# Recurrence of a block on one core: the projection of the answers goes between joins and transitions, that of the values into the scan

## The chip, the cores and the metric

The kernel runs on one core of a Trainium2 chip. The metric is device time in microseconds (us) of one launch, the median of the runs. All data is float32; a float32 matmul stands as two instructions in the trace.

## The reference

Two transformer blocks follow each other on 512 tokens of width 1024. The first mixes in a context of 256 tokens, with a recurrence of RWKV kind, a state-space branch and 16 experts; the second has a retention and a delta-rule mixer and 16 experts again. The change concerns only the recurrence of the first block, which runs in both directions over 16 heads of 64:

```python
r, k, v, xw, xa, xg = jnp.split(u, RW_SPLITS, axis=-1)      # u: projected tokens, after centred_shift
...
kk = (k * p['rw_kk']).astype(F32).reshape(b_, n, RW_HEADS, RW_HEAD)
kk = kk * lax.rsqrt(jnp.maximum(jnp.sum(kk * kk, axis=-1, keepdims=True), 1e-12))
k_eff = k[:, :, None] * (1 + (a - 1) * p['rw_ka'])
...
def step(s, inp):
    r_t, w_t, k_t, v_t, kk_t, a_t = inp
    sa = jnp.einsum('bhvk,bhk->bhv', s, -kk_t)
    s = s * w_t[:, :, None, :] + sa[..., None] * (kk_t * a_t)[:, :, None, :] + v_t[..., None] * k_t[:, :, None, :]
    return s, (jnp.einsum('bhvk,bhk->bhv', s, r_t) if with_output else None)
```

`r` is called the answers here, `k` the keys, `v` the values. The answers are needed for the 512 tokens alone, keys and values for context and tokens, 768 in all.

## The kernel before

The function `rwkv` works on 8 pairs of heads (PAIRS, 128 channels each). The 768 positions of a pair are cut into 12 chunks of 64 for each of the two directions: 24 units. The engines run programs of their own, written out by hand, and wait for each other by semaphores; nothing schedules them. One turn of the main loop computes the recurrence of pair c ("core") and prepares pair p = c + 1 ("prep"); a first turn, c = -1, only prepares, the last, c = 7, only computes. So seven turns do both.

On TensorE a turn goes through these phases:

- near: inner products of keys in each unit (L608), then the values turned (L622), the bonus (L746), and the answer of the pair before turned (`turn_y`, L616).
- keys 0 to 5: for each four units products with the answers (L635, L641) and transposes (L648, L651). Between them stand the projections of the next pair's keys, its small low-rank products (L577, L578) and `modulate` 0 to 3 (L598), which multiplies the conditioning vector into weights that two slots (`rw_mod_w`) bring in by turns, all eight summed in PSUM bank 1. VectorE meanwhile inverts the triangles by substitution (L987, L988) and masks the products of each four units (L970, L973, L975).
- the values' part (L660), `join_first` (L670), `join_second` (L681, L683), which put 32-wide inverses together into 64-wide ones with ScalarE's copies (L914 to L934) between them, `modulate` 4 to 7, and the sums for the key norm (`kk_sums`, L584).
- transitions: for q = 0 to 5 products `wu` (L692) and `mr` (L703), each followed by one matmul of a projection; at q = 2 also `kk_spread` (L591). Then `new_part` (L713), the gate's product (L820).
- the scan, steps 1 to 11, each in both directions: TensorE multiplies the state with the step's transition (L723), VectorE makes the new state (L1045), and TensorE's next step waits for it. Beside them stand products that only add to the answer (L729 in steps 1 to 8, L734 from step 4).

A projection is eight matmuls (k = 0 to 7) of a 128x128 piece of `rw_w` with 512 tokens or 256 context positions (L571). `project_part(j, part, k0, k1)` does k0 to k1 of it; j is 0 for answers, 1 for keys, 2 for values, part 0 for tokens, part 1 for context. ScalarE copies the finished sum with a scale (`centre`, L842), VectorE adds the neighbours on both sides (`neighbours`, L997, L998), and `fill` (L1027 to L1031) multiplies keys, gated keys and answers with the decay factors that ScalarE made in `factors` (L848 to L853). The factor of the answers stands in `e1`. `exponents` (L1003 to L1007) makes the exponents, `write_keys` (L1013 to L1020) the effective keys. near of the next turn waits for both `fill`s and the values' neighbours.

There is one buffer `rw_w` for the projections' weights. SyncE loads the next pair's as soon as all of `project_part(2, 1, ...)` is done (L512).

## Time and profile before

| what | us |
|---|---|
| median of 3 runs (lowest, highest) | 4329.08 (4328.28, 4329.16) |
| the profiled execution's own time | 4327.74 |
| its span | 4326.0 |
| TensorE busy, of the span | 3495.1 (81%) |
| VectorE busy | 1618.1 (37%) |
| ScalarE busy | 774.8 (18%) |
| the recurrence, from 133 to 1076 | 943 |
| TensorE busy in it | 830.4 |
| VectorE busy in it | 622.4 |
| ScalarE busy in it | 354.1 |

The recurrence takes 943 us of the span. TensorE's near phases start at 303.15, 415.99, 528.82 and so on, one every 112.8 us. The share of the whole page is an average over stages with other limits, so everything that matters for this change is read from one such turn, here mostly the one that ends at 528.82. In it TensorE works nearly without a break, and the question is what stands behind each of its few pauses.

### The profile page before, as it was taken

The page shows a single profiled execution, that of the slowest core. Times are in us where ns is not written, and L with a number is a line of the kernel's source. Part 1 is how long each engine was busy: PE and PEld are TensorE (multiplying, and loading weights), DVE is VectorE, ACT ScalarE, POOL GpSimd, SP SyncE. Part 2 cuts the span into 40 slices and gives each one's busy share as a digit, 9 for nine tenths or more (in the row PEclk, how much of TensorE's full clock was granted, in tenths as well). Part 3 has the DMA queues.
Part 4 walks back from the last instruction along what each step waited for, and adds up shares of the span by engine and source line. Part 5 has one row for each costly group of instructions (what it writes and reads, how often), then busy time and mean ns, then how long its engine had stood idle before and what let it go on. Part 6 is the DMA issues. An engine that isn't in the chain of part 4 may idle for free. (4 is left out here: it accounts for less than half of the span.)

```text
span 4326.0 us, 57405 instructions
## 1 busy us (share of the span) xinstructions
PE 3495.1 (81%) x24436; PEld 2129.8 (49%) x24436; DVE 1618.1 (37%) x3303; ACT 774.8 (18%) x1501; POOL 51.8 (1%) x72
## 2 busy tenths in 40 slices
PE   5799999997879888689956778858797888758994
PEld 2466666666545555434433322334444444347883
DVE  2466666665465674600122000022314132251112
ACT  1233433442121111200010000011212112100101
POOL 0000000000000000000000000000000000000000
PEclk7899999998889899899967999969898999858997
DMA  3121122212010000122036999731102010137884
GB/s 132 45 70 61 64 69 70 70 54 79 30 52 36 29 29 30 60 105 97 39 149 254 428 428 428 303 119 42 74 6 80 39 41 1 63 137 283 328 326 160
DMA packets 98023, 531.13 MB, mean 123 GB/s; under 512 B 33568, under 2 KB 36112, under 8 KB 72992
## 3 DMA queue, kind: packets, MB, share of 16 engines
q1 hardware_dynamic: 90912, 503.06, 29.8%
q0 software_dynamic: 4608, 16.78, 1.1%
q10 hardware_dynamic: 2304, 8.39, 0.5%
q8 instruction: 156, 2.56, 0.2%
q14 instruction: 43, 0.35, 0.0%
HBM read 500.85 MB, written 27.34 MB: 122 GB/s over the span
## 5 line engine op out<-in xcount | busy, mean ns | idle before, releaser
L1930 PE MATMUL ex_ps<-ex_ring,ex_xs 128*64 128x512 f32 x1024 | 242.7, 629 | 62.5 <-DMA ex_ring<-expert_slabs_in 59.4
L571 PE MATMUL rw_ps<-hT,rw_w 128*128 128x512 f32 (+1 forms) x640 | 256.9, 531 | 16.2 <-DMA rw_w<-rw_slabs_in 15.9
L2667 PEld LDWEIGHTS ge_ps<-ge_xeT,ge_ring 128*128 128x128 f32 x2048 | 232.7, 193 | 10.5 <-issue 10.5
L2667 PE MATMUL ge_ps<-ge_xeT,ge_ring 128*128 128x128 f32 x2048 | 233.0, 276 | 2.9 <-DVE ge_xeT L2725 2.9
L2164 PE MATMUL mh_ps<-mh_w,xmT 128*128 128x512 f32 x512 | 221.5, 593 | 8.6 <-ACT mh_sg L2187 8.6
L1315 PE MATMUL sg_ps<-hTp,sg_w 128*128 128x512 f32 x384 | 179.5, 623 | 27.9 <-PEq L61 27.9
L1930 PEld LDWEIGHTS ex_ps<-ex_ring,ex_xs 128*64 128x64 f32 x1024 | 88.2, 145 | 216.5 <-issue 214.7
L2164 PEld LDWEIGHTS mh_ps<-mh_w,xmT 128*128 128x128 f32 x512 | 96.9, 190 | 132.5 <-issue 120.5
L571 PEld LDWEIGHTS rw_ps<-hT,rw_w 128*128 128x128 f32 x640 | 112.5, 191 | 98.9 <-issue 72.9
L2155 PE MATMUL mh_ps<-xmT,mh_w_ahead 128*128 128x512 f32 x256 | 121.0, 637 | 22.4 <-PEq L61 22.4
L1315 PEld LDWEIGHTS sg_ps<-hTp,sg_w 128*128 128x128 f32 x384 | 76.5, 201 | 117.4 <-issue 116.4
L1930 PE MATMUL ex_ps<-ex_ring,ex_hidT 128*64 128x512 f32 x512 | 119.2, 620 | 16.2 <-DMA ex_ring<-expert_slabs_in 15.1
L1610 PE MATMUL mg_ps<-mg_pb,ybT 128*128 128x512 f32 x256 | 114.0, 604 | 17.4 <-DMA mg_pb<-proj_b_in 17.4
L2729 DVE TENSOR_TENSOR ge_hid<-ge_hid,ge_ps 128x512 f32<-128x512 f32 x16 | 11.0, 688 | 291.5 <-PE ge_ps L2667 291.5
L1989 DVE TENSOR_TENSOR ex_hid<-ex_hid,ex_ps 128x512 f32<-128x512 f32 x16 | 11.0, 687 | 291.5 <-PE ex_ps L1930 291.5
L1672 PE MATMUL po_ps<-po_w,po_mT 128*128 128x512 f32 x256 | 112.0, 600 | 4.2 <-DMA po_w<-w_out_in 4.2
L2676 PE MATMUL ge_ps<-ge_ring,ge_hid 128*128 128x512 f32 x256 | 113.7, 597 | 0.8 <-issue 0.8
L1359 DVE SCALAR_TENSOR_TENSOR sg_acc<-sg_ps,sg_par,sg_acc 128x510 f32<-128x510 f32 (+3 forms) x176 | 110.5, 628 | 6.3
L1325 PE MATMUL sg_ps<-sg_wz,hTp 128*128 128x512 f32 x256 | 110.5, 592 | 0.0
L2164 PE MATMUL mh_ps<-mh_w_ahead,xmT 128*128 128x512 f32 x256 | 110.5, 592 | 0.0
L1443 PEld LDWEIGHTS sg_ps<-sg_xdt,sg_diff 128*128 128x128 f32 x512 | 65.2, 197 | 64.2 <-DVE sg_diff L1518 60.4
L2155 PEld LDWEIGHTS mh_ps<-xmT,mh_w_ahead 128*128 128x128 f32 x256 | 52.1, 205 | 89.3 <-issue 89.3
(571 smaller groups left out, 5606.8 us busy)
## 6 DMA issues: line engine op xcount, KB each, us to landing
ex_ring<-expert_slabs_in SPq DMA_DIRECT2D x96, 2048.0 KB, 19.8
ge_ring<-expert_slabs_in SPq DMA_DIRECT2D x48, 2048.0 KB, 12.4
rw_mod_w<-mod_w_in SPq DMA_DIRECT2D x64, 384.0 KB, 4.0
rw_mod_w<-ada_in SPq DMA_DIRECT2D x64, 256.0 KB, 3.3
mh_w_ahead<-head_slabs_in SPq DMA_DIRECT2D x8, 2048.0 KB, 10.1
mh_w<-head_slabs_in SPq DMA_DIRECT2D x8, 2048.0 KB, 10.1
rw_w<-rw_slabs_in SPq DMA_DIRECT2D x8, 1536.0 KB, 6.3
sg_w<-xbc_slabs_in SPq DMA_DIRECT2D x4, 3072.0 KB, 9.9
```

The source lines that it names most:

```text
L571: mm = pe.matmul(where[j, part], w[:, k, P * j:P * j + P], tokens, start=k == 0, stop=k == KC - 1)
L1315: mm = pe.matmul(ps[:, bank, :], w[:, k, P * b:P * b + P], hTp[:, k, :], start=k == 0, stop=k == KC - 1)
L1325: mm = pe.matmul(ps[:, 6 + c % 2, :], hTp[:, k, P * c:P * c + P], wz[:, k, :], start=k == 0, stop=k == KC - 1)
L1359: link(dve.scalar_tensor_tensor(out[:, lo:hi], src[:, lo + j - 2:hi + j - 2], par[:, b, j:j + 1], out[:, lo:hi], ALU.mult, ALU.add))
L1443: mm = pe.matmul(ps[:, 7 * (c % 2), v], diff[:, n % ND, P * h:P * h + P], xdt[:, d, c, v], start=n % 4 == 0 and h == 0, stop=n % 4 == 3 an ...
L1610: mm = pe.matmul(ps[:, b + j, :], src[:, k, off + P * t:off + P * t + P], w[:, k, :], start=k == 0, stop=k == nk - 1)
L1672: mm = pe.matmul(ps[:, 4 + t, :], mT[:, k, P * t:P * t + P], w[:, n, k, :], start=k == 0, stop=k == KC - 1)
L1930: mm = pe.matmul(ps[halves[j], bank, :], src[:, k, halves[j]], ring[:, (n + j) % RING, k, :], start=k == 0, stop=k == KC - 1)
L2155: mm = pe.matmul(ps[:, b, :], w[0][:, k, P * b:P * b + P], xmT[:, k, :], start=k == 0, stop=k == KC - 1)
L2164: mm = pe.matmul(ps[:, 4 + t, :], xmT[:, k, P * t:P * t + P], w[1 + n // 4][:, k, :], start=k == 0, stop=k == KC - 1)
L2667: mm = pe.matmul(ps[:, 2 + 2 * (j % 2) + n, P * f:P * f + P], w[:, k, P * f:P * f + P], xeT[:, j, k, :], start=k == 0, stop=k == KC - 1)
L2676: mm = pe.matmul(ps[:, 6 + h, :], hid[:, j, f, :], w[:, f, 512 * h:512 * h + 512], start=f == 0, stop=f == FB - 1)
```

## The change

The projections of the next pair are dealt out differently on TensorE. The work is the same; only the order differs.

- The answers' projection, before 3 matmuls after keys 4, 2 before `join_first` and 3 before `join_second`, is now 2 before `join_second` and 6 in the transitions, one for each q.
- The values' projection over the tokens, before 6 in the transitions and 2 after the gate's product, is now one matmul in each of the scan steps 1 to 8. That over the context, before two in each of the steps 1 to 4, is now one in each of the steps 1 to 8.
- The wait for `mod_done` (VectorE has taken bank 1 away) stands ahead of the scan instead of ahead of the transitions, since bank 1 is where the values' tokens are summed.
- VectorE: the answers' neighbours come after scan step 1 instead of in the transitions; `fill` is cut in two, `fill` and `fill_answers`. The answers of direction 0 are filled after step 2, `write_keys(p, 1)` stands after step 3 instead of 2, both fills of direction 1 after step 8 instead of after step 10, the values' neighbours after steps 9 and 10 instead of 5 and 7.
- ScalarE: the answers' `centre` stands after the last `keep_wu`, and `factors(p, 1)` waits until the answers of direction 0 are filled, since it writes `e1` anew.

```diff
@@ TensorE, the main loop
                     if core:
                         keys(c, 4)
                         modulate(c, 2)
-                    if prep:
-                        project_part(0, 0, 0, 3)
-                    if core:
                         keys(c, 5)
                         modulate(c, 3)
                         value_part(c)
                         modulate(c, 4)
-                    if prep:
-                        project_part(0, 0, 3, 5)
-                    if core:
                         join_first(c)
                         modulate(c, 5)
                     if prep:
-                        project_part(0, 0, 5, 8)
+                        project_part(0, 0, 0, 2)
...
                         wu(c, 0)
                         wu(c, 1)
-                        pe.wait_ge(s.mod_done, c + 1)
                     for q in range(6):
...
-                            project_part(2, 0, q, q + 1)
+                            project_part(0, 0, q + 2, q + 3)
...
                     if prep:
-                        project_part(2, 0, 6, 8)
+                        if core:
+                            pe.wait_ge(s.mod_done, c + 1)
                         pe.wait_ge(s.kk_done, p + 1)
                     for step in range(1, RW_NCH):
                         if core:
                             scan_step(c, step)
-                        if prep and step <= 4:
-                            project_part(2, 1, 2 * step - 2, 2 * step)
+                        if prep and step <= 8:
+                            project_part(2, 0, step - 1, step)
+                            project_part(2, 1, step - 1, step)
@@ ScalarE
                     else:
+                        act.wait_ge(s.filled, 2 * p + 1)
                         act.activation(e1[:, :], ee[:, :], ACT.Exp, scale=KAPPA).then_inc(s.first_exp, 1)
...
                     if prep:
-                        centre(p, 0, 0, rc[:, :], ps[:, 2, :])
                         factors(p, 0)
                     if core:
                         for q in range(3, 6):
                             keep_wu(c, q)
                     if prep:
+                        centre(p, 0, 0, rc[:, :], ps[:, 2, :])
                         factors(p, 1)
@@ VectorE
-                    dve.tensor_tensor(bk[:, u, 64:P], token_cut(aas[:, d, :]), token_cut(bf[:, :]), ALU.mult)
+                    dve.tensor_tensor(bk[:, u, 64:P], token_cut(aas[:, d, :]), token_cut(bf[:, :]), ALU.mult).then_inc(s.keys_filled, 1)
+
+                def fill_answers(p, d):
+                    ul = slice(RW_NCH * d + RW_CC, RW_NCH * d + RW_NCH)
                     dve.wait_ge(s.shifted_r, p + 1)
-                    dve.tensor_tensor(kr[:, ul, 64:P], token_cut(rc[:, :]), token_cut(rf[:, :], RW_CC), ALU.mult).then_inc(s.filled, 1)
+                    dve.tensor_tensor(kr[:, ul, 64:P], token_cut(rc[:, :]), token_cut(e1[:, :], RW_CC), ALU.mult).then_inc(s.filled, 1)
...
                     if prep:
-                        neighbours(p, 0, 0, rc[:, :], ps[:, 2, :], SEQ)
-                        dve.sem_inc(s.shifted_r, 1)
                         dve.wait_ge(s.norm_spread, p + 1)
...
                         scan_step(c, 1)
+                    if prep:
+                        neighbours(p, 0, 0, rc[:, :], ps[:, 2, :], SEQ)
+                        dve.sem_inc(s.shifted_r, 1)
+                    if core:
                         scan_step(c, 2)
+                    if prep:
+                        fill_answers(p, 0)
+                    if core:
+                        scan_step(c, 3)
                     if prep:
                         write_keys(p, 1)
                     if core:
-                        for step in range(3, 6):
+                        for step in range(4, 9):
                             scan_step(c, step)
+                    if prep:
+                        fill(p, 1)
+                        fill_answers(p, 1)
+                    if core:
+                        scan_step(c, 9)
                     if prep:
                         neighbours(p, 2, 0, vc[:, CTX:NT], ps[:, 1, :], SEQ)
                     if core:
-                        scan_step(c, 6)
-                        scan_step(c, 7)
+                        scan_step(c, 10)
                     if prep:
                         neighbours(p, 2, 1, vc[:, 0:CTX], ps[:, 3, 256:512], CTX)
                         dve.sem_inc(s.shifted_v, 1)
-                    if core:
-                        for step in range(8, 11):
-                            scan_step(c, step)
-                    if prep:
-                        fill(p, 1)
```

TensorE from `modulate` 2 (L598) to the transitions, in a turn that does both, before and after. The L571 rows are projections; xN counts matmuls.

```order
 L651 MATMUL rw_ps<-consts,rw_kr 64x64 x8
 L598 MATMUL rw_ps<-rw_mod_w,rw_cond 32x320 x4
-L571 MATMUL rw_ps<-hT,rw_w 128x512 x3
 L635 MATMUL rw_ps<-rw_kr,rw_bk 64x128 x8
 L641 MATMUL rw_ps<-rw_kr,rw_bk 64x64 x8
```

```order
 L660 MATMUL rw_ps<-rw_tk 64x64 x48
 L598 MATMUL rw_ps<-rw_mod_w,rw_cond 32x320 x4
-L571 MATMUL rw_ps<-hT,rw_w 128x512 x2
 L670 MATMUL rw_ps<-rw_low,rw_mid 32x32 x48
 L598 MATMUL rw_ps<-rw_mod_w,rw_cond 32x320 x4
-L571 MATMUL rw_ps<-hT,rw_w 128x512 x3
+L571 MATMUL rw_ps<-hT,rw_w 128x512 x2
 L681 MATMUL rw_ps<-rw_diag,rw_mid 32x32 x24
```

Six projection matmuls of 512 columns leave the stretch between keys 4 and `join_second`. In the changed kernel the scan's lines are the same on TensorE (L723, L729, L734). Its start there, from the gate's product (L813 of the changed kernel) to step 3:

```order
L813 MATMUL rw_ps<-xg,rw_gw 128x512
L723 MATMUL rw_ps<-rw_kx,rw_tk 64x64 x2
L729 MATMUL rw_ps<-rw_tk 64x64 x4
L723 MATMUL rw_ps<-rw_kx,rw_tk 64x64 x2
L729 MATMUL rw_ps<-rw_tk 64x64 x4
L571 MATMUL rw_ps<-hT,rw_w 128x512
L571 MATMUL rw_ps<-hT,rw_w 128x256
L723 MATMUL rw_ps<-rw_kx,rw_tk 64x64 x2
L729 MATMUL rw_ps<-rw_tk 64x64 x4
L723 MATMUL rw_ps<-rw_kx,rw_tk 64x64 x2
L729 MATMUL rw_ps<-rw_tk 64x64 x4
```

Each of the steps 1 to 8 is now followed by a matmul of 512 and one of 256 columns, where steps 1 to 4 had two of 256. VectorE in the scan of the kernel before, from the states of steps 3 to 5 (two each, so x6) to the answer's statistics (L1126):

```order
L1045 SCALAR_TENSOR_TENSOR rw_kx<-rw_ps,rw_fac,rw_kx 128x64 x6
L997 SCALAR_TENSOR_TENSOR rw_v<-rw_ps,rw_par,rw_v 128x511
L998 SCALAR_TENSOR_TENSOR rw_v<-rw_ps,rw_par,rw_v 128x511
L1045 SCALAR_TENSOR_TENSOR rw_kx<-rw_ps,rw_fac,rw_kx 128x64 x4
L997 SCALAR_TENSOR_TENSOR rw_v<-rw_ps,rw_par,rw_v 128x255
L998 SCALAR_TENSOR_TENSOR rw_v<-rw_ps,rw_par,rw_v 128x255
L1045 SCALAR_TENSOR_TENSOR rw_kx<-rw_ps,rw_fac,rw_kx 128x64 x6
L1027 TENSOR_TENSOR rw_kr<-rw_kk,rw_q 128x12x64
L1028 TENSOR_TENSOR rw_bk<-rw_sg,rw_e 128x12x64
L1029 TENSOR_TENSOR rw_bk<-rw_a,rw_e 128x12x64
L1031 TENSOR_TENSOR rw_kr<-rw_r,rw_e 128x8x64
L1126 TENSOR_REDUCE rw_st<-rw_ps 128x8
```

The end of the scan on VectorE in the changed kernel, from step 4 on (L1043 is the state's line there, L1022 to L1029 the fills, L993 and L994 the neighbours):

```order
L1043 SCALAR_TENSOR_TENSOR rw_kx<-rw_ps,rw_fac,rw_kx 128x64 x10
L1022 TENSOR_TENSOR rw_kr<-rw_kk,rw_q 128x12x64
L1023 TENSOR_TENSOR rw_bk<-rw_sg,rw_e 128x12x64
L1024 TENSOR_TENSOR rw_bk<-rw_a,rw_e 128x12x64
L1029 TENSOR_TENSOR rw_kr<-rw_r,rw_e 128x8x64
L1043 SCALAR_TENSOR_TENSOR rw_kx<-rw_ps,rw_fac,rw_kx 128x64 x2
L993 SCALAR_TENSOR_TENSOR rw_v<-rw_ps,rw_par,rw_v 128x511
L994 SCALAR_TENSOR_TENSOR rw_v<-rw_ps,rw_par,rw_v 128x511
L1043 SCALAR_TENSOR_TENSOR rw_kx<-rw_ps,rw_fac,rw_kx 128x64 x2
L993 SCALAR_TENSOR_TENSOR rw_v<-rw_ps,rw_par,rw_v 128x255
L994 SCALAR_TENSOR_TENSOR rw_v<-rw_ps,rw_par,rw_v 128x255
L1129 TENSOR_REDUCE rw_st<-rw_ps 128x8
```

The four fills now stand between the states of step 8 and step 9, the values' neighbours behind the states of steps 9 and 10.

## Rows read from the trace of the kernel before

**Rows 1.** Waits of TensorE, 416 to 529: total us, times, longest.

```profile
PE rw_ps L635 <- DVE rw_kr L1152: 2.5, 1, 2.5
PE rw_ps L723 <- DVE rw_kx L1045: 2.1, 3, 0.9
```

**Rows 2.** Timeline of TensorE to the transitions: start, duration, [idle before, releaser].

```profile
459.50 2.84 PE L571 MATMUL rw_ps<-hT,rw_w 128*128 128x512 f32 x6
...
469.90 1.98 PE L571 MATMUL rw_ps<-hT,rw_w 128*128 128x512 f32 x4
...
474.13 2.84 PE L571 MATMUL rw_ps<-hT,rw_w 128*128 128x512 f32 x6
...
481.09 1.96 PE L692 MATMUL rw_ps<-rw_kx,rw_xt 64*64 64x128 f32 x32
...
489.47 1.60 PE L591 MATMUL rw_ps<-consts,rw_kk 128*128 128x128 f32 x12
```

**Rows 3.** Timeline of ScalarE in the joins.

```profile
473.57 0.58 ACT L921 COPY rw_mid<-rw_ps 32x512 f32<-32x512 f32 x1 [1.65 <-PE rw_ps L670]
...
475.31 2.11 ACT L925 COPY rw_xt<-rw_diag 32x384 f32<-32x384 f32 x4
...
478.56 1.95 ACT L934 COPY rw_xt<-rw_ps 32x384 f32<-32x384 f32 x4 [0.18 <-PE rw_ps L683]
```

**Rows 4.** Timeline of VectorE, last mask of the keys.

```profile
463.48 0.69 DVE L973 TENSOR_TENSOR rw_tk<-rw_ps,consts 128x512 f32<-128x512 f32 x1 [2.36 <-PE rw_ps L635]
```

**Rows 5.** Landing of the loads of rw_mod_w, whole run.

```profile
DMA to landing us min/median/max: 2.6/3.7/8.1
```

**Rows 6.** Timeline of VectorE in the transitions.

```profile
490.26 0.74 DVE L997 SCALAR_TENSOR_TENSOR rw_r<-rw_ps,rw_par,rw_r 128x511 f32<-128x511 f32 x1
...
491.93 0.75 DVE L1083 SCALAR_TENSOR_TENSOR rw_kk<-rw_k,rw_par,rw_ps 128x512 f32<-128x512 f32 x1
...
499.15 0.68 DVE L1031 TENSOR_TENSOR rw_kr<-rw_r,rw_e 128x512 f32<-128x512 f32 x1
...
505.07 1.88 DVE L1101 TENSOR_TENSOR rw_kx<-rw_ps,rw_fac 128x512 f32<-128x512 f32 x3
```

**Rows 7.** Timeline of TensorE, gate, scan and next near.

```profile
507.05 1.10 PE L820 MATMUL rw_ps<-xg,rw_gw 128*128 128x512 f32 x2 [1.80 <-issue]
...
509.79 0.33 PE L723 MATMUL rw_ps<-rw_kx,rw_tk 64*64 64x64 f32 x4
...
510.63 1.13 PE L571 MATMUL rw_ps<-hT,rw_w 128*128 128x256 f32 x4
...
516.33 0.33 PE L723 MATMUL rw_ps<-rw_kx,rw_tk 64*64 64x64 f32 x4 [0.75 <-DVE rw_kx L1045]
...
517.40 1.13 PE L571 MATMUL rw_ps<-hT,rw_w 128*128 128x256 f32 x4
...
528.82 2.42 PE L608 MATMUL rw_ps<-rw_kr,rw_bk 64*64 64x64 f32 x48 [2.87 <-DVE rw_kr L1031]
```

**Rows 8.** Timeline of VectorE in the scan.

```profile
512.63 0.95 DVE L1013 TENSOR_TENSOR rw_sg<-rw_kk,rw_a 128x768 f32<-128x768 f32 x1
...
515.99 0.48 DVE L1045 SCALAR_TENSOR_TENSOR rw_kx<-rw_ps,rw_fac,rw_kx 128x64 f32<-128x64 f32 x2
...
525.47 0.95 DVE L1027 TENSOR_TENSOR rw_kr<-rw_kk,rw_q 128x768 f32<-128x768 f32 x1
...
528.68 0.68 DVE L1126 TENSOR_REDUCE rw_st<-rw_ps 128x8 f32<-128x512 f32 x1
```

**Rows 9.** Stretches: length, busy (instructions) of PE, PEld, DVE, ACT, POOL, PEclk, DMA, GB/s.

```profile
392.00:416.00 24.00, 17.19 (x312) 12.77 (x306) 16.11 (x37) 3.39 (x6) 0.00 (x0) 1.00 0.19 68
...
416.00:430.00 14.00, 11.47 (x243) 10.42 (x243) 10.28 (x26) 9.39 (x22) 0.00 (x0) 0.77 0.12 27
```

**Rows 10.** Timeline of VectorE in the first turn, which only prepares.

```profile
169.17 0.17 DVE L1070 TENSOR_SCALAR rw_norm<-rw_ps 128x12 f32<-128x12 f32 x1 [2.42 <-PE rw_ps L584]
...
171.33 0.75 DVE L997 SCALAR_TENSOR_TENSOR rw_r<-rw_ps,rw_par,rw_r 128x511 f32<-128x511 f32 x1 [1.49 <-ACT rw_r L842]
```

5 lines of the change are left out of this document (2 added, 3 removed).

## The prediction, written before the changed kernel ran

> **What bounds the recurrence now.** I read first the share of busy time by stretch, then TensorE's waits, then the timelines of the three engines side by side through one turn. TensorE is the engine to watch: it is busy for 830 of the 943 us, VectorE for 622, ScalarE for 354. The turn takes 112.8 us from near to near (415.99 to 528.82, the last in [rows 7]). TensorE pauses in it before near (2.87, until VectorE's last fill), before the gate (1.80) [rows 7], before keys 0 (2.5) and in the scan (2.1 in three pieces) [rows 1]. That is some 9.3 of 112.8 us. Moving work on TensorE can only win by filling such a pause, and loses where it opens one. Two parts of the turn matter: the stretch from keys 5 to the transitions, which loses work, and the scan, which takes it.
>
> **Part 1, keys and joins.** Three projection matmuls between keys 4 and 5 go. They start at 459.50 and take 2.78 (three matmuls are x6 and 2.84, of which 0.06 overlaps) [rows 2]. Does VectorE hold keys 5 back instead? Its last mask waited 2.36 for TensorE's product [rows 4], so it is early; the mask that keys 5 need was done at about 458.2. So everything to the values' part comes 2.78 earlier, and VectorE 2.36. Before `join_first` two matmuls go (1.92, from 469.90), before `join_second` one of three (0.92 of 2.77, from 474.13) [rows 2]. TensorE could reach `join_second` 2.78 + 1.92 + 0.92 = 5.62 earlier.
>
> ScalarE is the next to be late. Its copies between the joins follow the values' part, which moves by 2.78, and only the wait of 1.65 before L921 gives way [rows 3]: `join_first` comes 4.70 earlier, so L921 starts 4.40 earlier (at 469.17, right behind the copies in front of it). That is 2.78 plus all but 0.03 of 1.65. L925 is then done with the rest at 4.40, and L934, which waited another 0.18, at 4.58 earlier: it ends at 480.51 - 4.58 = 475.93. The first `wu`, before at 481.09 [rows 2], needs it and starts near 476.0. **Gain 5.0**, and TensorE pauses about 0.5 there that it did not before. The bounds: 5.62 if ScalarE were no limit; 2.78 if L921's wait gave nothing.
>
> `modulate` 7 gets less time for its weights: its slot is reloaded once `modulate` 5 is done (about 469.4) and it is due at 473.5. With the second issue 0.5 later and a landing of 3.7 [rows 5] it is in at 473.6, and a delay of up to 0.5 is lost in ScalarE's limit anyway. I take nothing; the price is worked out below.
>
> **Part 2, transitions.** The six fillers stay six, of the same size. The wait for bank 1 costs nothing at either place, VectorE takes it before the first `wu`. What changes is VectorE's chain to the gate. The answers' neighbours leave it (490.26 to 491.93), but the key's norm cannot start before `kk_spread` is through, 489.47 + 1.5 = 491.0 [rows 2, 6], so 0.9 is won; the answers' fill leaves too, 499.15 to 499.87, 0.7 [rows 6]. VectorE is 1.6 earlier at its last three products. The third needs `new_part`, which ended at 507.05 - 1.80 = 505.25 [rows 7], and takes a third of 1.88 [rows 6], 0.65. So the gate's product starts at 505.25 + 0.1 + 0.65 + 0.1 = 506.1 in the old time, **gain 0.9**, with 1.6 and 0 as bounds.
>
> **Part 3, the scan.** In the old kernel it starts at 509.79 and near at 528.82 [rows 7]: 19.03. In the new one two matmuls of 512 no longer stand ahead of it (their time, 1.8, is counted here), so it starts at 507.05 - 5.0 - 0.9 + 0.93 (the gate) = 502.1.
>
> Step lengths on TensorE: 0.84 for steps 1 to 3 (509.79 to 510.63), 1.07 for step 4 (516.33 to 517.40), 0.98 for 5 to 8 [rows 7] (0.98 from the starts of later steps in the same timeline). Together 7.5. Each is followed by one matmul of 512, 0.91, and one of 256, 0.53 (517.40's four instructions are followed by the next step 1.07 later), so 8 x 1.44 = 11.5. Step 9 is reached at 19.0.
>
> VectorE beside it, from the scan's start: the state of a step is ready 0.45 + 0.28 after TensorE starts it. Neighbours of the answers, 1.6, between 1.0 and 2.6: step 2's product comes at 2.3 and its state is asked for at 2.75, no delay. `write_keys`, 3.36 (512.63 to 515.99 [rows 8]), from 5.65 to 9.0: the state of step 4 is then late, and TensorE may go on with step 5 at 9.0 + 0.34 (515.99 to 516.33 [rows 7, 8]) = 9.34. It gets there at 9.36. So this stall of 0.75 [rows 7] is just covered; if it isn't, it costs a few tenths. The same for the stalls of 0.9 and 0.4 after steps 6 and 8, whose causes move to the end.
>
> The end is VectorE's. Step 8 starts at 16.6, its states are made by 17.75, then the four fills 3.21 (525.47 to 528.68 [rows 8]) until 20.95. States of step 9, 0.4; values' neighbours, 1.57 (as the answers', [rows 6]); states of step 10, 0.4; the second neighbours, 1.0 with its signal 1.1. Near starts at 24.5. TensorE was done with step 9 at about 19.5: of the last 5.0 us it works one. Near comes at 502.1 + 24.5 = 526.6 against 528.82. So of the 5.9 of parts 1 and 2 and the 1.8 of the moved pair, the scan takes 5.4 back: **gain 2.3 a turn**. Bounds from the two sides: the scan without any pause, 19.0 + 1.5 for steps 9 to 11 = 20.5, gives 6.3; with the old pauses of 2.1 and 2.87 kept and the new ones on top, 26.5, it gives 0.3.
>
> ScalarE's new wait (`e1`) is over after step 2, and it has 2.5 us of factors to make before the fills at 17.75; cover 11 us. Queued behind it are only the values' copies, due at 18.7. SyncE: the load of the projections' weights starts when the context's values are done, 19.0 instead of 9 after the scan's start. It lands in about 6.3 us, near 25.5, and its first reader stands 14 us after near's start. No cost. POOL has nothing moved.
>
> **The first turn** only prepares and is VectorE's. Its wait of 2.42 for the key sums goes, since six matmuls no longer stand ahead of them; the 1.49 before the answers goes as well [rows 10], but VectorE must now wait some 2.5 for the norm to be spread. **Gain 1.5** (0 to 3.9). The last turn has no projections: nothing.
>
> Sum: 7 x 2.3 + 1.5 = 17.6.
>
> **The clock.** The stretch from 416 to 430 ran at a granted 0.77, the 24 us before at 1.00 [rows 9]: twice a turn TensorE falls to 1.2 GHz, once behind the pause of 2.87 and once behind that of 2.5, not behind 1.80. At most 0.23 x 14 = 3.2 us a turn are lost so. Now the pause before near is in pieces, about 1.9, 1.5 and 0.5, none as long as those that the drop followed, though close together; and the turn's phases shift. I take 0.6 a turn, 4 in all, between -1.6 (a third drop) and 3.2 a turn. The Trainium skill ("TensorE: Matmul & The Clock Gate", HAM oscillation) puts the return to the half clock down to long gaps between matmuls, and by that alone the drop before near would be gone: 1.6 x 7 = 11 us instead of 4. The same page (A second HAM failure mode) speaks against that: frequent short idles between groups also make the clock swing. No row of this trace has such a broken pause, so the sum keeps to the value near the lower end.
>
> The profiled execution took 4327.7, 1.3 under the median. 4327.7 - 17.6 - 4 = 4306.1 for it, **4307.5** at the median.
>
> **Rivals.**
> - *The clock gives more.* The drop behind the broken pause goes in all turns, and that behind keys' 2.5 in some: 1.6 to 2.6 a turn, 4329 - 17.6 - 15 = 4297. For it: no piece is as long as 2.5. Against: TensorE works only 1 of 5 us there. Chance 0.17.
> - *The joins don't shrink as far.* ScalarE and VectorE hold each other, 4.0 instead of 5.0 is won, `write_keys` just stalls step 5, a clock drop moves: gain 1.1 a turn, 4329 - 9 = 4320. Chance 0.12.
> - *Nothing comes of it.* The scan is a chain between two engines, and a projection in each step only makes it longer; what was won in front goes into the end, where VectorE has 7 us of work behind step 8 and TensorE nothing. If the tail is 2 us longer than I work out, the turn stays at 112.8: 4328. Against: the rows give each link of the tail. Chance 0.07.
> - *Slower, by the weights of `modulate` 7.* They decide from a landing of 6.4 us on (3.6 of room, 0.5 of slack, 2.3 of gain). The longest landing of all was 8.1, the median 3.7 [rows 5]. At 8.1 in every turn, 4.0 late, a turn loses 1.7: 4329 + 12 - 1.5 = 4339. Against: TensorE never waited more than tenths for them. Chance 0.05.
>
> **How the numbers follow.** The forecast has 0.59, its own range 4301 to 4315. The range of 8 in 10 goes from 4297, the clock's rival, to 4321, the weaker joins. 0.2% of 4329 is 8.7 us, about what a measurement of this kernel tells from none. Faster by more: below 4320.4, the forecast, the clock's rival and half of the weaker joins, less a little for the unknown: 0.83. Within: 0.11. Slower: 0.06.
>
> **What would show it.** In the changed profile near should follow near after about 110 us. The pause of 0.5 before the first `wu` (on ScalarE's L934), the gate's of 0.9, no pause in steps 1 to 8, then about 1.9 and 1.5 before steps 10 and 11 and 0.5 before near, all released by VectorE; the granted clock between near and keys 1 over 0.77. The forecast is wrong if step 5 or later steps stall, if `modulate` 7 waits for a DMA, or if the joins are less than 4 us nearer to keys 5.

## The result, and the profile after

The changed kernel takes 4332.6 us at the median of 20 runs (4320.6 to 4340.8). The kernel before, run beside it 20 times, takes 4324.8 (4319.0 to 4332.0). The ratio is 1.0017, with a 95% interval of 1.0009 to 1.0025: slower by 0.17%, where 4307.5 was forecast. The difference is small, but the interval leaves one out, and a repetition gave the same ratio.

| profiled execution | before | after |
|---|---|---|
| own time / span, us | 4327.7 / 4326.0 | 4336.5 / 4334.8 |
| mean granted clock of TensorE | 0.893 | 0.887 |
| to the first near | 193.9 | 193.8 |
| first near to eighth near (seven turns) | 786.0 | 786.4 |
| eighth near to the end | 3346.1 | 3354.6 |

In the seven turns that do both nothing was won. The last turn of the recurrence and the stages behind it, whose instructions are the same, took 8.5 us more; I come back to those at the end. The turns of before are alike (112.7 to 112.8, the first 109.2). Those of after are not. Each piece below is read from the starts of the first near, first `wu`, gate and next near in TensorE's timeline; "pause" is a pause there behind which no wait of before stands.

| turn | near to first `wu` | `wu` to gate | gate to near | turn | new pauses in the joins |
|---|---|---|---|---|---|
| before | 65.1 | 25.96 | 21.77 | 112.8 | none |
| 1 | 56.7 | 24.91 | 26.07 | 107.6 | 0.5 DMA |
| 2 | 62.5 | 26.48 | 26.07 | 115.1 | 0.86 and 0.17 unreleased, 0.5 DMA |
| 3 | 61.4 | 24.90 | 26.08 | 112.4 | 0.47 unreleased |
| 4 | 62.6 | 27.36 | 26.07 | 116.0 | 1.83 unreleased |
| 5 | 60.2 | 24.90 | 26.08 | 111.2 | 0.87 DMA |
| 6 | 60.3 | 24.90 | 26.08 | 111.3 | 0.5 DMA |
| 7 | 61.8 | 24.91 | 26.08 | 112.8 | 0.6 unreleased |

"Unreleased" means that the profile shows nothing that the engine waited for (its word is "issue"). The pause before the gate carries this word too, in both kernels [rows 7]; it is not counted here.

First TensorE's waits between 100 and 1090 us (total, times, longest). L813 is the gate, L723 and L734 are the scan's products, L608 is near, L598 is `modulate`, L670 and L683 are the joins. DVEq is VectorE's sequencer; at L1125 it signals that the values' neighbours are done.

```profile
PE rw_ps L635 <- DVE rw_kr L1155: 17.7, 7, 2.5
...
PE rw_ps L608 <- DVEq L1125: 12.2, 8, 7.6
PE rw_ps L723 <- DVE rw_kx L1043: 9.4, 7, 1.3
...
PE rw_ps L734 <- DVE rw_kx L1043: 8.9, 7, 1.3
PE rw_ps L813 <- issue: 6.7, 8, 0.8
...
PE rw_ps L598 <- DMA rw_mod_w<-mod_w_in: 3.0, 5, 0.9
...
PE rw_ps L598 <- issue: 1.8, 1, 1.8
...
PE rw_ps L683 <- issue: 1.1, 2, 0.6
...
PE rw_ps L670 <- issue: 0.9, 1, 0.9
```

Per turn the scan's waits are 1.34 and 1.27, the gate's is 0.84 (it was 1.80 [rows 7]), near's is at most 0.73 (2.87 [rows 7]), and that of keys 0 is unchanged [rows 1]. The last four lines are new: `modulate` waits for its weights (in four of the seven turns and once behind them), and it and the joins wait four times for nothing that is shown (a fifth such pause is the 0.17 of turn 2).

The end of the third turn's scan, TensorE's timeline (start, duration, instructions, [idle before, releaser]):

```profile
502.79 1.10 PE L813 MATMUL rw_ps<-xg,rw_gw 128*128 128x512 f32 x2 [0.84 <-issue]
503.82 0.33 PE L723 MATMUL rw_ps<-rw_kx,rw_tk 64*64 64x64 f32 x4
...
523.65 0.33 PE L723 MATMUL rw_ps<-rw_kx,rw_tk 64*64 64x64 f32 x4
...
525.67 0.33 PE L723 MATMUL rw_ps<-rw_kx,rw_tk 64*64 64x64 f32 x4 [1.34 <-DVE rw_kx L1043]
...
527.62 0.52 PE L734 MATMUL rw_ps<-rw_kx,rw_tk 64*64 64x64 f32 x8 [1.27 <-DVE rw_kx L1043]
528.87 0.91 PE L608 MATMUL rw_ps<-rw_kr,rw_bk 64*64 64x64 f32 x12 [0.73 <-DVEq L1125]
```

Steps 1 to 9 run without a pause, then come the three that were forecast. Near starts 25.05 after the scan's start.

The joins in the fourth turn, same view. L584 is the key sums, L692 is `wu`:

```profile
585.58 0.74 PE L598 MATMUL rw_ps<-rw_mod_w,rw_cond 128*32 128x320 f32 x6
588.15 1.24 PE L598 MATMUL rw_ps<-rw_mod_w,rw_cond 128*32 128x320 f32 x10 [1.83 <-issue]
589.32 2.23 PE L584 MATMUL rw_ps<-consts,rw_e 128*128 128x2 f32 x12
591.47 3.68 PE L692 MATMUL rw_ps<-rw_kx,rw_xt 64*64 64x128 f32 x32
```

and in the fifth, the best one:

```profile
702.97 0.75 PE L598 MATMUL rw_ps<-rw_mod_w,rw_cond 128*32 128x320 f32 x8 [0.87 <-DMA rw_mod_w<-mod_w_in]
703.64 1.50 PE L584 MATMUL rw_ps<-consts,rw_e 128*128 128x2 f32 x12
705.08 1.96 PE L692 MATMUL rw_ps<-rw_kx,rw_xt 64*64 64x128 f32 x32
```

The same 32 `wu` instructions take 3.68 in one turn and 1.96 in the other. The stretches of after (length, busy time and instructions of PE, PEld, DVE, ACT, POOL, then PEclk, DMA share, GB/s) say why:

```profile
392.00:416.00 24.00, 21.13 (x292) 13.69 (x288) 15.54 (x35) 3.58 (x6) 0.00 (x0) 1.00 0.15 56
416.00:430.00 14.00, 11.01 (x239) 10.11 (x240) 10.54 (x27) 9.40 (x22) 0.00 (x0) 0.74 0.17 45
...
585.00:589.00 4.00, 2.17 (x58) 1.06 (x51) 0.33 (x1) 3.23 (x6) 1.36 (x3) 1.00 0.15 57
589.00:597.00 8.00, 8.00 (x64) 6.99 (x62) 1.22 (x4) 2.91 (x5) 0.00 (x0) 0.57 0.08 21
```

Behind the pause of 1.83, TensorE works without a gap for 8 us at a granted 0.57, most of it at 1.2 GHz and not 2.4. Such a half-clock stretch lasts 6.8 here, and 3.4 in turn 2. Before had none between the one behind keys 0 and the next near. The two at near and behind keys 0 are still there. Before they were 3.4 long; in after that at near is 6.8 in turns 2 and 7, and that behind keys 0 is 6.8 in turn 3.

### The profile page after: what moved, and what is told of

It reads as the page before. It is cut to its first block and busy times, and to the rows that moved or that the text cites. A ratio compares the mean times of both kernels' runs of the same rounds, so it can differ in the third digit from the quotient of the medians.

```text
span 4334.8 us, 57412 instructions
## 1 busy us (share of the span) xinstructions
PE 3517.9 (81%) x24436; PEld 2142.7 (49%) x24436; DVE 1619.3 (37%) x3303; ACT 775.4 (18%) x1501; POOL 51.9 (1%) x72
## 5 line engine op out<-in xcount | busy, mean ns | idle before, releaser
L571 PE MATMUL rw_ps<-hT,rw_w 128*128 128x512 f32 (+1 forms) x640 | 263.2, 540 | 16.1 <-DMA rw_w<-rw_slabs_in 15.8
L571 PEld LDWEIGHTS rw_ps<-hT,rw_w 128*128 128x128 f32 x640 | 113.0, 194 | 101.0 <-issue 74.6
L1318 PEld LDWEIGHTS sg_ps<-hTp,sg_w 128*128 128x128 f32 x384 | 76.4, 200 | 117.1 <-issue 116.1
L1362 DVE SCALAR_TENSOR_TENSOR sg_acc<-sg_ps,sg_par,sg_acc 128x510 f32<-128x510 f32 (+3 forms) x176 | 110.5, 628 | 6.3
L1328 PE MATMUL sg_ps<-sg_wz,hTp 128*128 128x512 f32 x256 | 110.5, 592 | 0.0
L2167 PE MATMUL mh_ps<-mh_w_ahead,xmT 128*128 128x512 f32 x256 | 110.5, 592 | 0.0
## 6 DMA issues: line engine op xcount, KB each, us to landing
mh_w_ahead<-head_slabs_in SPq DMA_DIRECT2D x8, 2048.0 KB, 10.2
```

Source lines behind the costliest of these rows:

```text
L571: mm = pe.matmul(where[j, part], w[:, k, P * j:P * j + P], tokens, start=k == 0, stop=k == KC - 1)
L1318: mm = pe.matmul(ps[:, bank, :], w[:, k, P * b:P * b + P], hTp[:, k, :], start=k == 0, stop=k == KC - 1)
L1328: mm = pe.matmul(ps[:, 6 + c % 2, :], hTp[:, k, P * c:P * c + P], wz[:, k, :], start=k == 0, stop=k == KC - 1)
L1362: link(dve.scalar_tensor_tensor(out[:, lo:hi], src[:, lo + j - 2:hi + j - 2], par[:, b, j:j + 1], out[:, lo:hi], ALU.mult, ALU.add))
L2167: mm = pe.matmul(ps[:, 4 + t, :], xmT[:, k, P * t:P * t + P], w[1 + n // 4][:, k, :], start=k == 0, stop=k == KC - 1)
```

## The experiments

Three theories stood after the first profile. **A, the clock:** the wide matmuls that the change took from among the joins' narrow ones had kept the clock up, and in the scan's tail too little work is left between the pauses. **B, the chain:** the engines' dependences make the turn as long as it is, and the clock is beside the point. **C, the loads:** `modulate`'s weights, now due sooner, hold TensorE up in the joins, with a DMA or without a releaser. The expectations of 3, 5 and 6, written before those runs, call "theory B" what belongs to A here, that wide work between the joins' narrow matmuls keeps the clock up; the text keeps to the three meanings above. Ratios are to the kernel before on the same chip, with 95% intervals.

### 1. The changed kernel again

No edit.

> The changed kernel once more, unchanged, for a second profile. If its turns of the recurrence are long by chance events (half-clock stretches in mid-turn, pauses of TensorE that no engine releases), these will fall on other turns or have other sizes, while the clean turn stays at 111.2 us and the gate-to-near part at 26.1. If they belong to the order of instructions, the same turns (second and fourth) are long again, 115 and 116 us. Time 4325 to 4340. If the 7 us that the later stages lost in the first profile come from the change, they are there again; if not, the stages behind the recurrence take 3244 to 3251 either way.

Measured: 4336.0 against 4327.3, ratio 1.0017 (1.0007 to 1.0026). Turns: 107.9, 115.2, 112.9, 118.9, 112.5, 109.7, 113.0. The long ones are again the second and the fourth: they belong to the order of the instructions, the second branch of the expectation. In the fourth the pause stands between the same six and ten instructions of L598 as above:

```profile
587.93 0.74 PE L598 MATMUL rw_ps<-rw_mod_w,rw_cond 128*32 128x320 f32 x6
590.89 2.29 PE L598 MATMUL rw_ps<-rw_mod_w,rw_cond 128*32 128x320 f32 x10 [2.22 <-issue]
593.11 2.72 PE L584 MATMUL rw_ps<-consts,rw_e 128*128 128x2 f32 x12
595.76 3.68 PE L692 MATMUL rw_ps<-rw_kx,rw_xt 64*64 64x128 f32 x32
```

So the pause belongs to that instruction of that turn in the program, and its length (1.83, 2.22) to the execution. The sixth turn had no half-clock stretch behind keys 0 and took 109.7; the forecast was 109.9 (112.8 less 2.3 and 0.6). From the eighth near to the end this profile took 3350.1; the expectation's 3244 to 3251 is a slip for 3344 to 3351.

### 2. Spare matmuls in the pauses

One 128x512 matmul into a bank that nobody reads, behind scan steps 9 and 10 and in keys 0.

```diff
+                def filler():
+                    pe.matmul(ps[:, 6, :], hT[:, 0, CTX:CTX + P], hT[:, 0, CTX:NT], start=True, stop=True)
...
                         pe.wait_ge(s.v_kept, 2 * c + 2)
+                        filler()
...
                             project_part(2, 1, step - 1, step)
+                        if core and prep and step in (9, 10):
+                            filler()
```

> The changed kernel with three idle-time matmuls of 128x512 a turn whose result nobody reads: one behind scan step 9, one behind step 10 (pauses of 1.34 and 1.27 us), one ahead of keys 0's wait for the readout (pause of 2.5). Theory A, the clock eats the gain: the granted clock near the start of near and after keys 0 stays up, each turn gains 1 to 3 us, 7 to 20 us in all, so 4312 to 4325. Rival, the clock is a by-product and unreleased pauses decide: nothing gained, or slower by up to 0.3 us for each filler that doesn't fit, 4331 to 4338.

Measured: 4323.9, ratio 0.9992 (0.9981 to 1.0003), so 12 us less than the run of experiment 1 beside it. The pauses before steps 10 and 11 are 0.28 and 0.22. The half-clock stretch at near is gone in every turn, that behind keys 0 stays in turns 2, 3, 5, 6 and 7: 416 to 430 runs at 0.88, against 0.74 above.

```profile
416.00:430.00 14.00, 11.63 (x245) 8.85 (x241) 11.75 (x32) 10.00 (x24) 0.00 (x0) 0.88 0.24 63
```

Turns 3 to 5 take 111.0 to 111.6. Turns 2 and 7 (112.8, 112.7) still have a half-clock stretch behind the joins, and the sixth (116.1) one behind a DMA wait of 2.9 for `modulate`'s weights. The fourth has one in the joins, behind an unreleased pause of 1.27. This supports A for the tail, and leaves the joins.

The spare matmul of keys 0 did not come into its pause. It stands behind the wait for ScalarE's copies of the values and ahead of the wait for the readout, and the trace shows that the engine paused for the former (L595 is the spare matmul):

```profile
424.66 1.87 PE L595 MATMUL rw_ps<-hT 128*128 128x512 f32 x2 [2.37 <-ACT rw_tk L895]
```

The pause of 2.5 is still one of 2.4, in this run and in the others with spare matmuls there. So none of them tests what filling that pause would do.

### 3. Three projections back before keys 5

```diff
                         modulate(c, 2)
+                    if prep:
+                        project_part(0, 0, 0, 3)
+                    if core:
                         keys(c, 5)
...
-                    if prep:
-                        project_part(0, 0, 0, 2)
...
-                            project_part(0, 0, q + 2, q + 3)
+                            if q:
+                                project_part(0, 0, q + 2, q + 3)
```

> The changed kernel with the first three matmuls of the answers' projection back between keys 4 and 5, the other five in the transitions at q = 1 to 5, none between the joins. By my old sum: 2.78 is put back ahead of keys 5, 1.84 is taken away ahead of join_second and 0.9 at q = 0; the joins are ScalarE's, so a clean turn should be 1 to 2 us longer than 111.2. Theory B, the denser row of small matmuls in the joins makes the pauses that nobody releases and pulls the clock down in mid-turn: with still fewer large matmuls between the joins these pauses stay or grow, 4335 to 4345. If the stretch from keys 4 on is what matters, they get fewer, 4325 to 4333.

Measured: 4358.3, ratio 1.0067 (1.0055 to 1.0080), turns 2 to 7 of 116.0 to 119.3: the slowest kernel of all, and slower than either branch of the expectation. With nothing wide left between the joins, TensorE waits 1.2 to 1.5 for ScalarE in each turn, and a long half-clock stretch (10.2 to 13.7 us) begins there. Third turn:

```profile
483.89 0.85 PE L681 MATMUL rw_ps<-rw_diag,rw_mid 32*32 32x32 f32 x43 [1.52 <-ACT rw_mid L920]
...
485.95 0.85 PE L683 MATMUL rw_ps<-rw_mid,rw_diag 32*32 32x32 f32 x25 [0.83 <-issue]
486.74 2.36 PE L598 MATMUL rw_ps<-rw_mod_w,rw_cond 128*32 128x320 f32 x16
489.03 2.72 PE L584 MATMUL rw_ps<-consts,rw_e 128*128 128x2 f32 x12
491.68 3.68 PE L692 MATMUL rw_ps<-rw_kx,rw_xt 64*64 64x128 f32 x32
```

The stretches around it:

```profile
478.00:482.00 4.00, 4.00 (x160) 3.16 (x155) 3.75 (x6) 3.23 (x7) 0.00 (x0) 1.00 0.52 167
482.00:496.00 14.00, 11.65 (x186) 9.42 (x180) 4.00 (x7) 8.82 (x18) 1.36 (x3) 0.63 0.30 94
```

### 4. The spare matmuls in the kernel before

As in 2, with both of the tail's spare matmuls behind the last scan step, where the kernel before has its pause of 2.87.

> The kernel before with the same kind of matmuls: two behind the last scan step (pause of 2.87 us before near) and one ahead of keys 0's wait for the readout. Theory A: both half-clock stretches of a turn (3.4 us each, 1.7 lost in each at most) go or get rarer, 10 to 22 us faster than before, 4303 to 4315. If the half clock costs nothing because VectorE and ScalarE set the pace there, 4323 to 4327, as before.

Measured: 4325.6, ratio 0.9997 (0.9989 to 1.0006). One half-clock stretch instead of two, and turns of 112.2 instead of 112.8: the 1.7 us of clock that came back at near gave only 0.6 (0.4 against the profile of experiment 8). In the fourth turn, of 110.7, the second stretch was missing too, worth 1.5. So the two stretches don't cost the same; behind near the other engines seem to set the pace, which no run here tests by itself. And the spare matmuls are no gain by themselves: the 12 us of experiment 2 belong to the changed kernel.

### 5. Six spare matmuls where the six projections stood

The changed kernel, and dummies of the same size at the old places: three before keys 5, two before `join_first`, one before `join_second`.

```diff
                         modulate(c, 2)
+                        if prep:
+                            for _ in range(3):
+                                filler()
                         keys(c, 5)
...
                         modulate(c, 4)
+                        if prep:
+                            filler()
+                            filler()
                         join_first(c)
                         modulate(c, 5)
+                        if prep:
+                            filler()
```

> The changed kernel with six matmuls of 128x512, whose result nobody reads, exactly where the six of the answers' projection stood before: three between keys 4 and 5, two ahead of join_first, one behind modulate 5. That is three more a turn than the run with three put back (4358). Theory B, what holds the clock and spares the pauses is wide work between the narrow matmuls of the joins: no half-clock stretch in mid-turn, no unreleased pause, near to the first wu in 65.1 us as before the change, all turns alike at 116.1; 4348 to 4354, faster than with three matmuls less. Rival, a matmul costs its time and nothing else: 6 x 0.92 x 7 = 39 us over the changed kernel, 4370 to 4376; or, if drops and pauses stay beside it, more.

Measured: 4352.7, ratio 1.0053 (1.0040 to 1.0066). Turns 2 to 7 take 116.04 to 116.06, near to `wu` 65.05 to 65.07, as in before (65.1) and as expected. The joins run through at full clock; the dummies are L595:

```profile
482.12 1.13 PE L595 MATMUL rw_ps<-hT 128*128 128x512 f32 x2
483.08 1.88 PE L571 MATMUL rw_ps<-hT,rw_w 128*128 128x512 f32 x4
484.89 0.85 PE L684 MATMUL rw_ps<-rw_diag,rw_mid 32*32 32x32 f32 x42
...
486.43 1.28 PE L601 MATMUL rw_ps<-rw_mod_w,rw_cond 128*32 128x320 f32 x16
...
489.08 1.96 PE L695 MATMUL rw_ps<-rw_kx,rw_xt 64*64 64x128 f32 x32
```

and the stretch that ran at 0.63 in experiment 3:

```profile
480.00:494.00 14.00, 14.00 (x312) 9.99 (x307) 4.49 (x8) 10.16 (x19) 1.36 (x3) 1.00 0.27 86
```

TensorE has six matmuls (5.5 us) a turn more to do than in experiment 3, and is 1.2 us a turn faster (seven turns 808.8 against 817.5, one profile each; the intervals of the two ratios overlap, and the runs were on two chips). Theory B alone can't make that. Two things come with the spare matmuls, and this run does not part them: wide work between the narrow, and no pause in the joins, since TensorE now comes to ScalarE's copies later. Nor is there an unreleased pause in the seven turns, though the loads of theory C are all there. It also shows what the changed scan and transitions do with the joins held as they were: 116.05 against 112.8, 3.2 a turn lost, which the gain of 4.9 in the joins must first pay.

### 6. One projection put before the key sums

The third of the six answers' matmuls goes back from the transitions to behind `modulate` 7.

```diff
                     if prep:
+                        if core:
+                            project_part(0, 0, 2, 3)
                         kk_sums(p)
...
-                            project_part(0, 0, q + 2, q + 3)
+                            if q or not core:
+                                project_part(0, 0, q + 2, q + 3)
```

> The changed kernel with one matmul of the answers' projection (k = 2) moved from the transitions (q = 0) to behind modulate 7, ahead of kk_sums, where TensorE had about 0.5 us to spare. Theory B: one wide matmul among 128x320 and 128x2 ones keeps the clock up there in some turns; mid-turn half-clock stretches go from three turns in seven to one or none, gain 2 to 6 us: 4327 to 4333. Rival, one is too little or stands behind the place where the clock has already fallen: within 2 us of the changed kernel, 4331 to 4337, with q = 0 bare up to 0.3 us a turn slower.

Measured: 4332.1, ratio 1.0005 (0.9996 to 1.0014). `wu` to gate falls to 24.36, but the turns stay uneven: 118.9 in the fourth, with an unreleased pause of 2.28, again between the sixth and the seventh instruction of the same L598, and a half-clock stretch of 10.2 there. The median lies in the ranges of both theory and rival, so this run decides nothing between them.

### 7. Experiments 2 and 6 together, twice

> The run before this one and the three fillers of the earlier run (behind scan steps 9 and 10, ahead of keys 0's wait) together. If both kinds of half-clock stretch are independent, the gains add: 12 us from the fillers and 2 to 6 from the moved matmul, 4316 to 4322, some 7 us faster than the kernel before. If the moved matmul does nothing: 4322 to 4326.

> The fastest kernel so far once more, unchanged, beside the two others on one chip: 4314 to 4322, and about 0.2% faster than the kernel before again; at 4325 or more the first result was chance.

Measured: 4317.8, ratio 0.9977 (0.9968 to 0.9986), and the second time 4319.8, 0.9984 (0.9974 to 0.9994). Turns 2 to 7 take 109.6 to 111.6 in both. This is faster than both kernels, though the DMA waits for `modulate`'s weights are still there (0.2 to 1.2 a time). The half-clock stretch behind keys 0 is missing in three or four of the turns 2 to 7, though its pause is not; why, was not settled.

### 8. The kernel before again

> The kernel before once more, unchanged, for a second profile of it: its turns 112.8 us each with two half-clock stretches of 3.4 us, no pause that nobody releases. From near of the last turn to the end the first profile had 3346 us, the two of the changed kernel 3355 and 3350. If the later stages vary by chance, this one may lie anywhere from 3342 to 3355; if the change slows them, 3343 to 3348.

Measured: 4328.0, ratio 0.9996 (0.9987 to 1.0005). Turns 2 to 7 are at 112.4 to 112.6, with two half-clock stretches of 3.4 us each and no unreleased pause in the joins. The unevenness of the turns is the changed kernel's own. The kind of pause is not: experiment 4, with the order of before, has an unreleased one of 2.18 at `modulate` in the last turn, where no projection stands in the joins.

### 9. Without the loads of `modulate`'s weights

Left out: all but the first two pairs of the 64 loads, so that the modulation is computed from old weights. TensorE's waits for these loads go with them.

```diff
                         if n >= SLOTS:
-                            sp.wait_ge(s.mod_used, n - SLOTS + 1)
+                            continue
...
-                    pe.wait_ge(mod_in[k % SLOTS], 32 * (n // SLOTS) + 32)
+                    if n < SLOTS:
+                        pe.wait_ge(mod_in[k % SLOTS], 32)
```

> The changed kernel without the loads of modulate's weights beyond the first two (62 of 64 pairs of DMAs left out, TensorE multiplies what stands in the slots, so the modulation's values are wrong); all instructions of TensorE, VectorE and ScalarE stay. In the recurrence these loads are the traffic beside which the pauses in the joins fall. Theory C, the pauses that nobody releases (0.5 to 2.3 us, at L670, L683, L598) are the instruction supply held up by these loads: they go, with them the waits for the weights and the mid-turn half-clock stretches; turns of 109.5 to 111.2, 4315 to 4324. Rival, the supply is short because the joins' narrow matmuls are used up faster than they can be brought, loads or none: the pauses in turns 2 and 4 stay at 1 to 2 us, 4326 to 4334.

Measured: 4318.4, ratio 0.9978 (0.9969 to 0.9987). In turns 1 to 7 no DMA wait and no unreleased pause is left in the joins. The fourth turn:

```profile
584.78 1.28 PE L599 MATMUL rw_ps<-rw_mod_w,rw_cond 128*32 128x320 f32 x16
...
587.89 1.96 PE L693 MATMUL rw_ps<-rw_kx,rw_xt 64*64 64x128 f32 x32 [0.40 <-ACT rw_xt L931]
```

The 16 instructions of L599 are in one piece, and in front of `wu` now stands the wait for ScalarE that the forecast had there. What is uneven still is the stretch at near: the turns in which it is 3.4 long take 110.4 and 110.5, those with 6.8 take 111.7 to 112.2. The first turn has one of 3.4 in its middle, behind a pause of 0.40 alone. C holds for the joins' pauses, and A for the tail.

The traces also show by what way the loads act. The page of the profile lists a DMA queue of the kind "instruction":

```profile
q8 instruction: 156, 2.56, 0.2%
```

Its packets are of 16 KB. In the seven turns of after there are 97 of them, one for every 254 matmuls and weight loads of TensorE (24618). Each of the 37 unreleased pauses that lie between 100 and 1090 us in ten of the profiles ended 1.27 to 1.59 us after such a packet did. (The profiles of experiments 8 and 9 and that of before have none.) In the fourth turn of after the packet ended at 586.86 and the pause at 588.15. That packet started when TensorE had begun 12560 matmuls and weight loads since the first near; in experiment 9 the same packet started at 12346, 214 of them earlier. In the 3 us before it the queue of the bulk loads (q1) had moved 311 packets, and none in experiment 9.

So these pauses are TensorE waiting for its next instructions, whose packet came late beside the loads of `modulate`'s weights. That q8 serves TensorE is read from its rate and from these times. Before has the same loads and no such pause, and this packet started at 12366 there. That its wide matmuls in the joins make the instructions at hand last longer, until the packet is in, is argued; experiment 5 fits it.

### 10. The one projection a place earlier

As experiment 7, but the third projection between `modulate` 6 and 7, so that it covers the weights' landing.

```diff
                         modulate(c, 6)
+                        if prep:
+                            project_part(0, 0, 2, 3)
                         modulate(c, 7)
```

> The fastest kernel so far (fillers and one matmul of the answers' projection behind modulate 7, 4317.8) with that matmul one place earlier, between modulate 6 and 7. If the wait of 0.5 to 1.2 us for modulate 7's weights counts, the matmul of 0.9 now stands in it: 0.5 us a turn, 3 to 4 us, 4313 to 4316. If ScalarE's copies set the first wu anyway, nothing: 4316 to 4320.

Measured: 4308.3 (4306.0 to 4313.0, 5 runs), ratio 0.9956 (0.9942 to 0.9970), the best kernel of all, and faster than either branch of the expectation. In the seven turns the DMA waits are gone, and the unreleased pauses in the joins are at most 0.5. The fourth turn:

```profile
579.79 0.75 PE L601 MATMUL rw_ps<-rw_mod_w,rw_cond 128*32 128x320 f32 x8
580.47 1.12 PE L571 MATMUL rw_ps<-hT,rw_w 128*128 128x512 f32 x2
581.52 0.75 PE L601 MATMUL rw_ps<-rw_mod_w,rw_cond 128*32 128x320 f32 x8
582.20 1.50 PE L584 MATMUL rw_ps<-consts,rw_e 128*128 128x2 f32 x12
583.63 1.97 PE L696 MATMUL rw_ps<-rw_kx,rw_xt 64*64 64x128 f32 x32
```

This turn has no half-clock stretch at all, neither at near nor at the joins:

```profile
524.00:538.00 14.00, 11.65 (x249) 8.85 (x250) 11.74 (x31) 10.26 (x24) 0.00 (x0) 1.00 0.26 62
...
582.00:596.00 14.00, 13.56 (x178) 10.67 (x174) 5.71 (x13) 8.53 (x12) 0.00 (x0) 1.00 0.05 12
```

Turns 2 to 7 take 110.1 to 110.5, but for the third with 112.9, whose stretch behind keys 0 is 6.8 long. Seven turns take 773.3, 12.7 less than before. But in the profiles of experiment 7 they take 773.7 and 773.9, so the 9.5 and 11.4 us between the medians do not show as turns that the one place made shorter. One profile a run does not tell where they come from.

## Why the prediction was wrong

The prediction said 20 us less for the seven turns (7 x 2.3 and 4 for the clock), measured were 0.4 more. Two steps failed: the clock, which was to give 0.6 a turn and took more than before, and the weights of `modulate`, which were put at nothing. By its own steps:

**Part 1, keys and joins.** Forecast 5.0, measured 4.9 in turns 5 and 6 (65.1 to 60.2 and 60.3). Right in its size. But the pause of 0.5 on ScalarE's copy did not show up: in turn 5 that copy (L930) was done by 704.41, and `wu` started at 705.08, since `modulate` 7 had waited 0.87 for its weights. **"I take nothing"** was the second step that failed. `modulate` waited for a DMA in four of seven turns, 0.48 to 0.87, which costs up to 0.7 a turn: without the loads the best turns need 59.4 to 59.6 there. The prediction had named such a wait as a sign of being wrong.

**Part 2, transitions.** Forecast 0.9, measured 1.06; the gate's pause is 0.84 where 0.9 stood. Right.

**Part 3, the scan.** The pauses came at their places, steps 2 to 9 don't stall, and `write_keys` is just covered. A step with its matmuls of 512 and 256 takes 2.33 and from step 4 on 2.57, where 2.28 and 2.42 were worked out, so step 9 is reached at 19.83 and not 19.0. VectorE's tail is nearly as forecast, and near starts at 25.05 instead of 24.5: 0.6 a turn less gain. Pauses of 1.34 and 1.27 stand where 1.9 and 1.5 were expected, because TensorE came later.

With the clock as it was in before, a turn was to take 110.5. Turns 5 and 6 took 111.2 and 111.3, and the two turns of experiment 9 with stretches like before's 110.4 and 110.5. So the sum of the instructions was sound to 0.8 us with the loads and to 0.1 without them. The 0.1 is in part luck: there the joins gave 5.7 and not 5.0, which makes up for the 0.6 of the scan.

**The first turn**, which only prepares, gained 0.1 and not 1.5. Its clock fell behind the pause of 0.98 that the key sums now have: 167 to 173 ran at a granted 0.50. The four instructions behind them took 2.42, and `kk_spread` (L591), after a pause of 0.74, took 2.93; before these took 1.96 and 1.58. VectorE waited for it. TensorE's timeline of after:

```profile
163.90 1.50 PE L584 MATMUL rw_ps<-consts,rw_e 128*128 128x2 f32 x12 [0.98 <-ACT rw_e L924]
165.26 2.42 PE L571 MATMUL rw_ps<-hT,rw_w 128*128 128x512 f32 x4
168.43 2.93 PE L591 MATMUL rw_ps<-consts,rw_kk 128*128 128x128 f32 x12 [0.74 <-ACT rw_kk L940]
```

and VectorE, which would have resumed about 170.0 by the forecast's 2.5 for spreading the norm:

```profile
171.40 0.75 DVE L1079 SCALAR_TENSOR_TENSOR rw_kk<-rw_k,rw_par,rw_ps 128x512 f32<-128x512 f32 x1 [3.89 <-PE rw_ps L591]
```

**The clock** is the step that failed most. It took a gain of 0.6 a turn, with a third stretch at half clock as its far bound (-1.6). It looked for pauses only at near and at keys 0, and asked which of these might heal. The change also took the wide matmuls out of a stretch of small ones, keys 5 to `modulate` 7, where a pause of about a microsecond can now make the clock fall (0.86 and 0.48 in turn 2, 1.83 in turn 4), and does not always (1.03 in the third turn of experiment 1). And the broken pause at near did not heal: its half-clock stretch is there in turns 2 to 7, 3.4 to 6.8 long, and 416 to 430 ran at 0.74, where it had been 0.77 [rows 9]. Experiments 3 and 5 show the first: with six spare wide matmuls at the joins' old places the clock stays up there, and the turns are shorter than with six fewer. Experiments 2 and 4 show the second, since spare matmuls in the pauses of the tail take that stretch away.

The clock's own record in the traces sums it up, for turns 2 to 7 (from the second near to the eighth):

| kernel | us | of these at half clock |
|---|---|---|
| before; again (8) | 676.7; 675.4 | 41; 41 |
| after; again (1) | 678.7; 682.3 | 61; 68 |
| after without the loads (9) | 668.6 | 54 |
| spare matmuls in the tail and keys 0 (2) | 675.5 | 34 |
| three back before keys 5 (3) | 704.2 | 110 |
| before with spare matmuls (4) | 671.6 | 17 |
| six spare matmuls in the joins (5) | 696.3 | 41 |
| one at the key sums (6) | 684.2 | 73 |
| 7, twice | 664.3; 664.5 | 10; 10 |
| 10 | 664.5 | 17 |

At half clock at most half of the time is lost. By that the clock took up to 10 us more from the six turns than before, where the forecast had 3.6 less.

The Trainium skill ("TensorE: Matmul & The Clock Gate", A second HAM failure mode) says that frequent micro-idles between groups of matmuls make the clock swing. By that the change would win nothing in the tail. The trace agrees: pauses of 1.34, 1.27 and 0.73 with 0.7 and 0.5 us of work between them went with the half clock, for 3.4 us in turns 3 to 6 and for 6.8 in turns 2 and 7.

The 20.4 us missing in the seven turns are these: 7.3 in six turns that are 1.2 longer than forecast even at their best (0.6 scan, 0.6 of clock that was not given), 11.8 in turns 2, 3, 4 and 7 (and 0.1 in turn 6) above 111.2, and 1.3 in turn 1. Read against turn 5 piece by piece, the 11.8 are of two kinds. From the values' part on, turns 2 and 4 lose 2.6 and 4.9, to their pauses and the half clock behind them. Ahead of the values' part turns 2, 3 and 7 lose 1.3, 1.4 and 1.6: these are the turns whose half-clock stretch at near or behind keys 0 is 6.8 long.

What stood as the rival on the other side, **slower by the weights of `modulate` 7**, named the right place and the wrong price. In this kernel's profiles the landings never were late enough to cost 4 us; in experiment 2 one was, where a wait of 2.85 went with a turn of 116.1. What cost was the clock behind short pauses, and a kind of pause that the rival did not know: unreleased, up to 2.2 us, next to the loads and gone without them.

**What stays open.** The seven turns were 0.4 us longer in one profile of the changed kernel and 4.3 in the other, against the profile of before, but the median is 7.8 longer. The rest lies behind the eighth near, in work that is the same. Some 1.5 of it is the last turn of the recurrence, 87.7 and 87.5 us long in the two profiles and 86.1 in both of before: it too has a wait for `modulate`'s weights (0.7) and longer half-clock stretches. In all that part took 3346.1 and 3348.5 in two profiles of before, 3354.6 and 3350.1 in two of after, and 3337.9 to 3348.8 in the nine others. Behind the recurrence, with one profile a run, I can't tell chance from an effect. Why the stretch at near is 3.4 long in some turns and 6.8 in others was not settled, nor whether it is the wide work itself or the missing pause that keeps the clock up in the joins.

## What to carry to other kernels

A matmul that is moved off a stretch of small ones takes its cover with it: before moving, list every pause and every load that comes due in that stretch, and price each at what TensorE then does at half clock, not only at its own length. Where an engine's tail of pauses can't be filled by useful work, a spare wide matmul into an unread bank may keep the clock, but its worth is what the engines behind it can use (0.6 of 1.7 us behind near, 1.5 behind keys 0). When turns that should be alike differ by microseconds, tabulate them one by one before reasoning on means: the best turn here was 1.2 us longer than forecast, two others 5.1 and 6.1. And where an engine pauses amid equal instructions with no releaser, put the packets of the instruction queue beside the pause: a bulk load that falls together with many small instructions can hold the next ones up.

## What the runs showed of the hardware

- Half-clock stretches in the seven turns had one of four lengths, about 3.4, 6.8, 10.2 and (twice, experiment 3) 13.7 us, each at a granted 0.5. Pauses of 0.86 and 0.48 in the joins were enough ahead of one (turn 2).
- TensorE paused for 0.2 to 2.3 us with no releaser in the profile, in the middle of a run of equal instructions, at the same instruction of the same turn in three executions (the fourth turn's L598, after six instructions: 1.83, 2.22 and, in experiment 6, 2.28). Each of the 37 such pauses ended 1.27 to 1.59 us after a 16 KB packet of the instruction queue. With the 256 and 384 KB loads left out there was none.
- A kernel with more work was faster: experiment 5 has 42 matmuls of 512 more than experiment 3, and its seven turns are 8.7 us shorter (5.6 us at the medians).
